# Three-layer forward pass on one core: finer first loads and another order of small work at the seams and in the last layer

## The chip, the cores and the metric

The kernel runs on one core of one Trainium2 chip. The metric is the device time of one execution in microseconds. The core has TensorE (PE, matmuls), VectorE (DVE), ScalarE (ACT), GpSimd (POOL) and SyncE (SP), which run side by side and wait for each other through semaphores; SP and POOL start transfers that 16 DMA engines carry out.

## The reference

One batch, T = 256 positions, width D = 2048, everything in f32. Two blocks of the form

```
h = rmsnorm(x, g0);  m = mixer(h);  x = x + rmsnorm(m, g1)
h = rmsnorm(x, g2);  f = relu(h @ w1)^2 @ w2;  x = x + rmsnorm(f, g3)
```

The first block's mixer is `z = h @ w_in` (2048 to 6144), a short convolution over three columns, a long two-sided convolution with filters that a small network makes (`sin` of `emb @ w1`, `@ w2`, `@ w3`, times a window), gates, and `@ w_out`. The second block's mixer subtracts centred means and multiplies by four 512x512 weights. The third layer is a hybrid attention: after a norm, one wide product gives the inputs of 8 MLA heads (low-rank queries and keys, rotary part), 4 NSA heads (compressed, selected and windowed keys) and 4 heads that attend to a memory of 256 rows. Each head's output is multiplied by `silu(z)`, the 16 heads' 2048 columns go through `w_out_2`, and the sum with x, scaled by a last norm, is the output.

## The kernel before, in words

All of the weights, some 400 MB, stream through the core once, as tiles of 128x2048 f32 (1 MB), which SP loads in the order of use into a ring of `NS = 4` slots raw0 to raw3 (`load_tile`, L962). ScalarE rounds a tile to its high part hi (L484), VectorE subtracts and keeps the low part raw_r (L604), and TensorE multiplies the columns of x, which are split in high and low too, in three products per pair: hi·high, hi·low, low·high (L341). A tile of 512 output columns gives 24 matmuls of 128x512: 4 rows of blocks (k), 2 halves of the positions (t), 3 products. `gemm` (its loop ends at L1152) runs them; `take` and `release` load the tile four ahead and split the tile `AHEAD = 2` further on.

Everything that isn't a product of weights is put between the products by hand. Small functions stand in the lists `later` and `extra`; `step()` calls the next one, at each tile's end and, with `steps=2`, after the second k as well. A function that is called there emits its instructions on every engine at that point of each engine's program. `release(j)`, which stands ahead of that step, emits the split of the tile further on first, unless `hold` says otherwise: then the split is emitted by the next `take`, behind the step's work. In `gemm` a true `hold` holds the last tile of a product alone.

Parts that the change touches:

- The start (L1373 to L1449). TensorE multiplies zeros (`warm`, the count is 4; each product of zeros is two matmuls in the profile) until the first data come. SP loads blocks of x^T (`first_block`, tile R_g) and the first two weight tiles in halves (`first_tile`, `load_piece`, L965). ScalarE and VectorE make for each block of 128 rows first the column of x (R_h<-R_g,cols: L480, L591), then the quarter tile (raw, 128x512). `last_rows` waits for x and issues the filters' tables on POOL (semaphore c6: w_f3, c_win and c_dft, 2 MB together).
- The seams, where one layer's sum becomes the next one's x: `x_columns` (L1244) with `residual` (L1350). With P a product in PSUM, the residual gives X (L591, 128x512 pieces), TensorE turns X (L344), ScalarE and VectorE scale the turned blocks into R_h, high part and low part. The first weight tile of the next layer is split in quarters between these (`quarter`). `gained(t)` multiplies the fourth piece of the sum with its gain (R_m, L588). The seams come at about 402 us (the first block's MLP) and 1908 us (the last layer), each time with the same calls.
- The last layer. Products w_i3 to w_i6 give the heads' inputs; the products w_i9, w_i10, w_i7 and w_i8 (`z_group`, L2091) give silu(z). Between them the heads are computed in steps, each head in three parts over three steps: scores (P<-R_s,R_f and the like), maximum and exponential (DVE L853 and L591 with masks, L858 without; ACT L557, L564), turns of them (L344, EV), a copy (ACT L480), values, and the scaled output R_m (DVE L591). `cmp_out` finishes the compressed keys.
- The last product, `w_o2`, reads the heads' gated outputs, turned by TensorE four heads at a time in the order `blocks` (L2266), the same as the order of its weights' rows.

Of the kernel before, what the change touches and what calls it, by code (L numbers as in the profile page):

```python
# [71 lines left out]
def col(v):  # L72
# [14 lines left out]
    [(4876, 5388)],  # L87
]
Z_ORDER = [8, 9, 10, 11, 2, 3, 4, 5, 6, 7, 0, 1]


def laid_out(i):
    o = dict(shape_constants())
# [27 lines left out]
    wo = i["w_out_2"][0]  # L121
    o["w_o2"] = tile_w(np.concatenate([wo[1024:], wo[:1024]], 0), 512)
    o["x"] = np.ascontiguousarray(i["x"][0].reshape(2, 128, 4, 512).transpose(2, 1, 0, 3))
# [4 lines left out]
    g = i["norm_g"]  # L128
# [347 lines left out]
class Act(Engine):  # L476
# [5 lines left out]
    def split(self, k, d, hi, raw, low, apart=False):  # L482
        self.wait_ge(("loaded", k) if k > 1 else ("loaded", k, d // 2))
        self.e.activation(hi, raw, ACT.Copy).then_inc(*self.inc("high_made", ("high", k, d)))  # L484
# [472 lines left out]
class Sync(Engine):  # L957
# [6 lines left out]
    def load_piece(self, k, d, o, i):  # L964
        self.e.dma_start(o, i).then_inc(*self.landed(f"w{2 * k + d}", ("loaded", k, d)))  # L965

# [24 lines left out]
def conduct(E, plan, listing):  # L991
# [122 lines left out]
    def gemm(name, xh, xl, x_names, nk, c, k0=0, steps=1, hold=False, lead=False, tail=False, late=False):  # L1114
# [19 lines left out]
        for group in groups:  # L1134
# [6 lines left out]
            for ts in turns:  # L1141
                for q, j, wh, wl in blocks:
                    for k in range(4):
                        for t in ts:
                            product(q, j, wh, wl, k, t)
                        if k == 1 and steps > 1:
                            step(steps - 1)
                    if ts[-1] == 1:
                        release(j, done[1], hold and q == n - 1)
                    if steps:  # L1150
                        step()
# [92 lines left out]
    def x_columns(res, th, tl, gain, filler=None):  # L1244
# [41 lines left out]
        if filler is None:  # L1286
# [8 lines left out]
            out_of(1)  # L1295
            quarter(3)
            first, second = early(0)
            first()
            squares_of(1)
            gained(0)  # L1300
            start(1, second)
            fetch(0, (1,))
            fetch(1, (1,))
            fetch(2)
            at_["pause"] = True
# [71 lines left out]
    b, k, warmed = bank(), ev(), mark("warm")  # L1377
    E.warm(b, k, 4, mark("zero"), warmed)
    bank_free[b] = ev_free[k] = [warmed]
    E.halves(half_m)  # L1380

    def first_tile(k, d):
        q = slice(1024 * d, 1024 * d + 1024)
        E.load_piece(k, d, m.raw[k][:, q], a["w_z"][k][:, q])
# [642 lines left out]

    extra += [cmp_last, nop, cmp_sums, nop, nop, cmp_turn, nop, cmp_out]

# [47 lines left out]

    banks, done = gemm("w_i3", HH, HL, h_m, 16, 512, steps=2)
    flush()
# [11 lines left out]
    def z_group(name, n, onto=False, between=None):  # L2091
        banks, done = gemm(name, HH, HL, h_m, 16, 512, steps=2)
        if between is not None:
# [133 lines left out]
    def mla_heads():  # L2227
        def over():
# [9 lines left out]
    banks, done = gemm("w_i4", HH, HL, h_m, 16, 512, steps=2)  # L2238
    flush()
# [5 lines left out]
    later.append(lambda: qnsa_m.extend(turn_plain(ks4, ms4, 128, 4, m.QNSA[:, 0:4, :], 96, [list(kpe_m), list(blk_m.values())], more=vw_m)))  # L2245
    banks, done = gemm("w_i5", HH, HL, h_m, 16, 384, steps=2)
    flush()
# [4 lines left out]
    extra += [lambda h=h: head_step(nsa(h, 1)) for h in range(4)] + [cmp_softmax, head_step, head_step, cmp_turned, lambda: cmp_values(0), lambda: cmp_values(1)]  # L2252
    banks, done = gemm("w_i6", HH, HL, h_m, 16, 512, steps=2)
    flush()
# [10 lines left out]

    blocks = [8, 9, 10, 11, 12, 13, 14, 15, 0, 1, 2, 3, 4, 5, 6, 7]  # L2266

    class Heads:
# [5 lines left out]
        def __getitem__(self, g):  # L2274
            return [o_m[blocks[self.k0 + 4 * g + h], t] for h in range(4) for t in range(2)]

    def heads_of(k0, n, th, tl, after=None):
        return columns(lambda t, c: ZO[:, t, 128 * blocks[k0 + c]:128 * blocks[k0 + c] + 128], Heads(k0), n, th, tl, th_free=after)

# [19 lines left out]
    for g in range(4):  # L2299
# [16 lines left out]
        if g < 3:  # L2316
            for t in range(2):
# [6 lines left out]
SEMAPHORES = (["product_done", "turn_done", "high_made", "act_done", "low_made", "dve_done", "pow_done", "row0", "row1", "stored"]  # L2324
              + [f"ring{k}" for k in range(NS)] + [f"w{k}" for k in range(4)] + [f"xt{c}" for c in (0, 2, 4, 6, 8, 12)] + [f"x{g}" for g in range(4)] + [f"c{k}" for k in range(17)])

# [68 lines left out]
```

## Time and profile before

| | us |
|---|---|
| median of 3 runs | 2354.55 (2353.98 to 2354.76) |
| profiled execution | 2354.21 |
| its span, first to last instruction | 2352.4 |
| TensorE busy | 2337.4 (99%), 10,945 matmuls |
| VectorE busy | 1304.2 (55%) |
| ScalarE busy | 1081.8 (46%) |
| transfers | 446.07 MB, mean 190 GB/s |

The granted clock of TensorE was 0.999 of full over the span. The span is what the timeline and the waits are counted in; the execution's own time is 1.8 us longer. TensorE's record of a matmul includes its pipeline, so records of neighbours overlap; a row "x2" in a timeline is two such that follow each other without a gap. An idle field in brackets is the time in which the engine had nothing to do ahead of the group, with the instruction that ended it.

### The profile page before, as it was taken

How to read it: one execution, taken by the hardware profiler on the slowest of the kernel's cores; microseconds unless marked ns; L12 is line 12 of the kernel's file. 1: busy time of each engine (PE TensorE's matmuls, PEld its weight loads, DVE VectorE, ACT ScalarE, POOL GpSimd, SP SyncE). 2: the span in 40 equal slices, each digit the busy share in tenths (PEclk: the TensorE clock that was granted, in tenths of full speed). 3: DMA queues.
4: the chain of work that ended last, by engine and by line, in shares of the span. 5: the costliest groups of instructions: out<-in, count | busy, mean ns of one | idle time of the engine just before them, and what ended most of it. 6: DMA issues, size and time to landing. Idle time of an engine off the chain costs nothing.

```text
span 2352.4 us, 25298 instructions
## 1 busy us (share of the span) xinstructions
PE 2337.4 (99%) x10945; PEld 1932.0 (82%) x10945; DVE 1304.2 (55%) x1330; ACT 1081.8 (46%) x1174; POOL 27.0 (1%) x46
## 2 busy tenths in 40 slices
PE   9999999999999999999999999999999999999998
PEld 7778788888888888888888888888888888888887
DVE  6655855544544554546864454544544575456654
ACT  6344444544344344354664444344344364444443
POOL 0000000000000000000000000000000010000000
PEclk9999999999999999999999999999999999999999
DMA  8444555655555555555555555555555555644444
GB/s 326 161 161 179 179 198 196 211 183 195 183 212 184 191 188 188 196 180 207 206 197 192 183 192 185 193 186 190 196 180 196 185 177 210 245 161 146 150 153 143
DMA packets 64159, 446.07 MB, mean 190 GB/s; under 512 B 7241, under 2 KB 7572, under 8 KB 12527
## 3 DMA queue, kind: packets, MB, share of 16 engines
q1 hardware_dynamic: 61568, 429.58, 51.6%
q0 software_dynamic: 2336, 14.76, 1.7%
q8 instruction: 86, 1.41, 0.2%
q14 instruction: 25, 0.20, 0.0%
q10 hardware_dynamic: 144, 0.12, 0.0%
HBM read 442.33 MB, written 2.10 MB: 189 GB/s over the span
## 4 chain that ended last, share of the span: by engine, by line
PE 94%; DMA 2%; ACT 2%; DVE 1%; issue 1%; SPq 0%; POOL 0%; ACTq 0%; POOLq 0%
PE P L341 92%; PE P L344 3%; DMA raw<-in_w_i 1%; ACT hi L484 1%; DMA raw<-in_w_z 1%; DVE raw_r L604 1%; ACT EV L510 0%; ACT EV L480 0%; DVE R_m L588 0%; SPq L969 0%; DVE R_h L591 0%; DVE X L591 0%; ACT EV L564 0%; ACT EV L557 0%; ACT R_h L480 0%
## 5 line engine op out<-in xcount | busy, mean ns | idle before, releaser
L604 DVE TENSOR_TENSOR raw_r<-raw,hi 128x2048 fp32r<-128x2048 f32 (+3 forms) x417 | 912.5, 2190 | 946.6 <-ACT hi L484 945.5
L484 ACT ACTIVATE hi<-raw 128x2048 fp32r<-128x2048 f32 (+3 forms) x417 | 763.8, 1833 | 1011.0 <-DMA raw<-in_w_d 388.1
L341 PE MATMUL P<-hi,R_h 128*128 128x512 f32 (+2 forms) x3840 | 1225.0, 393 | 1.5 <-DVE R_h L591 1.1
L341 PEld LDWEIGHTS P<-hi,R_h 128*128 128x128 f32 x3840 | 720.4, 188 | 153.5 <-issue 7.7
L341 PE MATMUL P<-hi,R_f_r 128*128 128x512 f32 x2480 | 776.9, 391 | 0.0
L341 PE MATMUL P<-raw_r,R_h 128*128 128x512 f32 (+2 forms) x1920 | 744.7, 388 | 0.0
L341 PEld LDWEIGHTS P<-hi,R_f_r 128*128 128x128 f32 x2480 | 465.5, 188 | 96.5 <-issue 0.3
L341 PE MATMUL P<-raw_r,R_f_r 128*128 128x512 f32 x1240 | 482.6, 389 | 0.0
L341 PEld LDWEIGHTS P<-raw_r,R_h 128*128 128x128 f32 x1920 | 361.0, 188 | 73.2 <-issue 4.3
L341 PEld LDWEIGHTS P<-raw_r,R_f_r 128*128 128x128 f32 x1240 | 232.9, 188 | 47.5
L344 PE MATMUL P<-ident,EV 128*128 128x128 f32 (+1 forms) x476 | 71.4, 272 | 0.7 <-ACT R_s L480 0.5
L588 DVE TENSOR_TENSOR R_m<-P,R_m 128x512 f32<-128x512 f32 x112 | 71.8, 682 | 0.0
L344 PEld LDWEIGHTS P<-ident,EV 128*128 128x128 f32 (+1 forms) x476 | 58.0, 139 | 14.8 <-issue 2.0
L588 DVE TENSOR_TENSOR R_f_r<-P,R_f_r 128x512 fp32r<-128x512 f32 x66 | 45.0, 684 | 0.0
L540 ACT ACTIVATE EV<-P,st 128x512 f32<-128x512 f32 x64 | 42.8, 669 | 0.0
L542 ACT ACTIVATE EV<-EV 128x512 f32<-128x512 f32 x64 | 40.5, 633 | 2.0
L510 ACT ACTIVATE EV<-X 128x512 f32<-128x512 f32 x48 | 29.9, 633 | 23.2 <-DVE X L588 20.2
L480 ACT ACTIVATE R_f_r<-P 128x512 fp32r<-128x512 f32 x66 | 38.0, 578 | 1.7 <-PE P L344 1.7
L557 ACT ACTIVATE EV<-EV,STAT 128x256 f32<-128x256 f32 (+1 forms) x32 | 14.6, 456 | 51.1 <-DVE STAT L853 51.1
L510 ACT ACTIVATE EV<-R_m 128x512 f32<-128x512 f32 x24 | 15.0, 626 | 34.3 <-DVE R_m L588 34.3
L480 ACT ACTIVATE R_h<-P,cols 128x128 fp32r<-128x128 f32 (+1 forms) x64 | 21.4, 432 | 16.5 <-PE P L344 16.4
L341 PE MATMUL P<-R_f,R_s 65*128 65x512 f32 (+5 forms) x96 | 27.8, 418 | 0.0
(190 smaller groups left out, 768.4 us busy)
## 6 DMA issues: line engine op xcount, KB each, us to landing
raw<-in_w_u SPq DMA_DIRECT2D x128, 1024.0 KB, 4.8
raw<-in_w_d SPq DMA_DIRECT2D x128, 1024.0 KB, 4.8
raw<-in_w_z SPq DMA_DIRECT2D x46, 1024.0 KB, 4.9
raw<-in_w_i SPq DMA_DIRECT2D x36, 1024.0 KB, 4.8
raw<-in_w_mo SPq DMA_DIRECT2D x16, 1024.0 KB, 4.8
raw<-in_w_o SPq DMA_DIRECT2D x16, 1024.0 KB, 4.8
raw<-in_w_mkv SPq DMA_DIRECT2D x8, 1024.0 KB, 4.7
R_g<-in_rows POOLq DMA_DIRECT2D x6, 1024.0 KB, 5.3
```

The source lines that it names most:

```text
L341: return self.e.matmul(o, l, r, start=start, stop=stop, skip_group_check=True)
L344: return self.e.transpose(o, i, self.m.ident[0:i.shape[0], 0:i.shape[0]])
L480: self.e.activation(o, i, ACT.Copy, **scale).then_inc(*self.inc("act_done", done))
L484: self.e.activation(hi, raw, ACT.Copy).then_inc(*self.inc("high_made", ("high", k, d)))
L510: self.e.activation(dst, src, ACT.Square, accum_out=o, **scale).then_inc(*self.inc("act_done", done))
L540: self.e.activation(o, p, ACT.Relu, scale=r).then_inc(*self.inc("act_done", evacuated))
L542: self.e.activation(o, o, ACT.Square).then_inc(*self.inc("act_done", done))
L557: self.e.activation(E[:, o:o + n], E[:, o:o + n], ACT.Exp, bias=S[:, t:t + 1], accum_out=S[:, 2 + t:3 + t]).then_inc(*self.inc("act_done", ...
L588: self.e.tensor_tensor(o, a, b, op).then_inc(*self.inc("dve_done", *done))
L604: self.e.tensor_tensor(low, raw, hi.bitcast(f32), ALU.subtract).then_inc(*self.inc("low_made", *names))
```

## The change

It has five parts. (1) At the start there are three products of zeros in place of four; the first weight tile comes in four quarters of 256 KB, the first of them ahead of x^T, and for this tile the quarter is split ahead of x's column. (2) The filters' tables are issued by a step of their own, one step later, and wait for the ninth weight tile ("loaded", 8) and no longer for x alone. (3) At the seams the fourth weight quarter is split behind the first turned blocks, and `gained(0)` stands behind four pieces of X. (4) In the last layer w_i3 to w_i6 and the z groups are held at every tile (`hold="all"`), and `cmp_out` stands behind the scores of the first MLA head. (5) The heads' order in the last product is NSA, MLA 0 to 3, memory, MLA 4 to 7, where it was NSA, memory, MLA.

```diff
+HEAD_ORDER = [8, 9, 10, 11, 0, 1, 2, 3, 12, 13, 14, 15, 4, 5, 6, 7]
...
-    o["w_o2"] = tile_w(np.concatenate([wo[1024:], wo[:1024]], 0), 512)
+    o["w_o2"] = tile_w(np.concatenate([wo[128 * h:128 * h + 128] for h in HEAD_ORDER], 0), 512)
...
                     if ts[-1] == 1:
-                        release(j, done[1], hold and q == n - 1)
+                        release(j, done[1], hold == "all" or hold and q == n - 1)
...
             out_of(1)
-            quarter(3)
             first, second = early(0)
             first()
+            quarter(3)
             squares_of(1)
-            gained(0)
             start(1, second)
             fetch(0, (1,))
             fetch(1, (1,))
+            gained(0)
             fetch(2)
...
-    E.warm(b, k, 4, mark("zero"), warmed)
+    E.warm(b, k, 3, mark("zero"), warmed)
...
     def first_tile(k, d):
-        q = slice(1024 * d, 1024 * d + 1024)
+        n = 1024 if k else 512
+        q = slice(n * d, n * d + n)
...
-    first_block(0, 0, 2)
     first_tile(0, 0)
+    first_block(0, 0, 1)
+    first_tile(0, 1)
+    first_block(0, 1, 1)
+    first_tile(0, 2)
     first_block(0, 2, 2)
-    first_tile(0, 1)
+    first_tile(0, 3)
...
         first_rows(3)
-        side_load("c6", m.f_w3, a["w_f3"], x_m[3])
+
+    def filter_tables():
+        side_load("c6", m.f_w3, a["w_f3"], ("loaded", 8))
...
         for c in range(4):
-            first_column(4 * g + c)
             q = slice(512 * c, 512 * c + 512)
-            E.split(g, c, m.hi[g][:, q], m.raw[g][:, q], m.low[g][:, q], True)
+            if g == 0:
+                E.split(g, c, m.hi[g][:, q], m.raw[g][:, q], m.low[g][:, q], True)
+                first_column(c)
+            else:
+                first_column(4 * g + c)
+                E.split(g, c, m.hi[g][:, q], m.raw[g][:, q], m.low[g][:, q], True)
...
-    later += [nop, last_rows, half_squares, nop, first_norm]
+    later += [nop, last_rows, half_squares, nop, first_norm, filter_tables]
...
-    banks, done = gemm("w_i3", HH, HL, h_m, 16, 512, steps=2)
+    banks, done = gemm("w_i3", HH, HL, h_m, 16, 512, steps=2, hold="all")
...
-        return [lambda h=h: head_step(mla(h)) for h in range(8)] + [head_step, over]
+        heads = [lambda h=h: head_step(mla(h)) for h in range(8)]
+        return heads[0:1] + [cmp_out] + heads[1:] + [head_step, over]
...
-    blocks = [8, 9, 10, 11, 12, 13, 14, 15, 0, 1, 2, 3, 4, 5, 6, 7]
```

The same `hold="all"` stands in the gemms of w_i4, w_i5, w_i6 and of `z_group`; `Heads` and `heads_of` use `HEAD_ORDER`. The changed kernel's lines stand one and more below those of the kernel before.

Three places show what moved. First SP's queue at the start of the program; raw is the first weight tiles, R_g holds x^T. Before:

```order
L969 DMA R_g<-in_xt 128x512
L965 DMA raw<-in_w_z 128x1024
L969 DMA R_g<-in_xt 128x512
L965 DMA raw<-in_w_z 128x1024
```
and in the changed kernel:

```order
L966 DMA raw<-in_w_z 128x512
L970 DMA R_g<-in_xt 128x256
L966 DMA raw<-in_w_z 128x512
L970 DMA R_g<-in_xt 128x256
L966 DMA raw<-in_w_z 128x512
L970 DMA R_g<-in_xt 128x512
L966 DMA raw<-in_w_z 128x512
L970 DMA R_g<-in_xt 128x512
```
The first 256 KB of weights now stand at the head of the queue, and the blocks of x^T behind them are of one, one and two columns of 256.

Second VectorE at the seam near 1908 us, from the residual's last product on; raw_r is the fourth quarter's low part, R_h the scaled turned blocks, st the sums of squares and the norm. Before:

```order
L588 TENSOR_TENSOR R_m<-P,R_m 128x512
L604 TENSOR_TENSOR raw_r<-raw,hi 128x396
L591 SCALAR_TENSOR_TENSOR R_h<-P,cols,R_h 128x128 x4
L588 TENSOR_TENSOR R_m<-R_m,R_g 128x512
L627 TENSOR_REDUCE st<-st 128x1
L596 TENSOR_SCALAR st<-st 128x1
L591 SCALAR_TENSOR_TENSOR R_h<-P,cols,R_h 128x128 x4
L588 TENSOR_TENSOR st<-st 128x1
L591 SCALAR_TENSOR_TENSOR st<-st 128x1 x2
L591 SCALAR_TENSOR_TENSOR X<-R_m,st,X 128x512 x4
L591 SCALAR_TENSOR_TENSOR R_h<-P,cols,R_h 128x128 x8
```
and in the changed kernel:

```order
L589 TENSOR_TENSOR R_m<-P,R_m 128x512
L592 SCALAR_TENSOR_TENSOR R_h<-P,cols,R_h 128x128 x4
L605 TENSOR_TENSOR raw_r<-raw,hi 128x396
L628 TENSOR_REDUCE st<-st 128x1
L597 TENSOR_SCALAR st<-st 128x1
L592 SCALAR_TENSOR_TENSOR R_h<-P,cols,R_h 128x128 x4
L589 TENSOR_TENSOR st<-st 128x1
L592 SCALAR_TENSOR_TENSOR st<-st 128x1 x2
L592 SCALAR_TENSOR_TENSOR X<-R_m,st,X 128x512 x2
L589 TENSOR_TENSOR R_m<-R_m,R_g 128x512
L592 SCALAR_TENSOR_TENSOR X<-R_m,st,X 128x512 x2
L592 SCALAR_TENSOR_TENSOR R_h<-P,cols,R_h 128x128 x8
```
The quarter went from ahead of the first R_h to behind them, and the second R_m from ahead of the norm to between the X. The seam near 402 us has the same order now; before, its quarter stood ahead of its R_h as well, with no R_m between.

Third VectorE at the memory heads; raw_r is a weight tile's low part, STAT the maxima and sums of the scores, R_m<-P,STAT,R_m a head's output. Before:

```order
L604 TENSOR_TENSOR raw_r<-raw,hi 128x2048
L858 TENSOR_REDUCE STAT<-P 128x2
L596 TENSOR_SCALAR STAT<-STAT 128x2
L864 RECIPROCAL STAT<-STAT 128x2
L858 TENSOR_REDUCE STAT<-P 128x2
L596 TENSOR_SCALAR STAT<-STAT 128x2
L591 SCALAR_TENSOR_TENSOR R_m<-P,STAT,R_m 128x128 x2
L864 RECIPROCAL STAT<-STAT 128x2
L604 TENSOR_TENSOR raw_r<-raw,hi 128x2048
```
and in the changed kernel:

```order
L859 TENSOR_REDUCE STAT<-P 128x2
L597 TENSOR_SCALAR STAT<-STAT 128x2
L865 RECIPROCAL STAT<-STAT 128x2
L605 TENSOR_TENSOR raw_r<-raw,hi 128x2048
L859 TENSOR_REDUCE STAT<-P 128x2
L597 TENSOR_SCALAR STAT<-STAT 128x2
L592 SCALAR_TENSOR_TENSOR R_m<-P,STAT,R_m 128x128 x2
L865 RECIPROCAL STAT<-STAT 128x2
```
Before, the low part stands ahead of the maximum of the next head's scores; now it stands behind that maximum and its reciprocal.

## Rows read from the trace of the kernel before

**Rows 1.** The page, section 1: busy us (share of the span) and instructions of each engine.

```profile
PE 2337.4 (99%) x10945; PEld 1932.0 (82%) x10945; DVE 1304.2 (55%) x1330; ACT 1081.8 (46%) x1174; POOL 27.0 (1%) x46
```

**Rows 2.** TensorE's waits over the whole span: engine, line, releaser, us, times, longest.

```profile
PE P L344 <- DVE R_m L591: 0.9, 1, 0.9
```

**Rows 3.** Timeline of TensorE, 0 to 10 us: start, duration, engine, operation, idle before.

```profile
1.46 3.78 PE L341 MATMUL P<-EV 128*128 128x512 f32 x4 [1.46 <-DVE half L613]
5.03 2.66 PE L341 MATMUL P<-EV 128*128 128x512 f32 x4
7.45 0.47 PE L341 MATMUL P<-hi,R_h 128*128 128x512 f32 x1
```

**Rows 4.** Timeline of VectorE at the start of the program.

```profile
6.61 0.69 DVE L604 TENSOR_TENSOR raw_r<-raw,hi 128x512 fp32r<-128x512 f32 x1 [1.29 <-ACT hi L484]
```

**Rows 5.** Windows of the start: us, busy of each engine, PEclk, DMA share, GB/s.

```profile
5.00:10.00 5.00, 5.00 (x16) 3.04 (x15) 2.99 (x6) 3.19 (x7) 0.35 (x1) 1.00 1.01 364
```

**Rows 6.** Timeline of ScalarE, 16 to 31 us.

```profile
16.70 0.63 ACT L484 ACTIVATE hi<-raw 128x512 fp32r<-128x512 f32 x1 [2.12 <-DMA raw<-in_w_z]
...
26.33 1.90 ACT L484 ACTIVATE hi<-raw 128x2048 fp32r<-128x2048 f32 x1
```

**Rows 7.** Timeline of TensorE, 28 to 32 us.

```profile
30.60 0.50 PE L341 MATMUL P<-hi,R_h 128*128 128x512 f32 x1 [0.23 <-DVE raw_r L604]
```

**Rows 8.** Timeline of TensorE, the first matmul that reads the filters' tables.

```profile
68.86 1.02 PE L341 MATMUL P<-R_f,R_s 65*128 65x512 f32 x2
```

**Rows 9.** Timeline of ScalarE at the two seams.

```profile
401.04 1.14 ACT L480 ACTIVATE R_h<-P,cols 128x128 fp32r<-128x128 f32 x4 [3.46 <-PE P L344]
...
1906.74 1.14 ACT L480 ACTIVATE R_h<-P,cols 128x128 fp32r<-128x128 f32 x4 [2.71 <-PE P L344]
```

**Rows 10.** Timeline of VectorE at the two seams.

```profile
401.69 1.13 DVE L591 SCALAR_TENSOR_TENSOR R_h<-P,cols,R_h 128x128 fp32r<-128x128 f32 x4 [0.83 <-ACT R_h L480]
402.74 0.68 DVE L588 TENSOR_TENSOR R_m<-P,R_g 128x512 f32<-128x512 f32 x1
...
407.85 2.15 DVE L591 SCALAR_TENSOR_TENSOR R_h<-P,cols,R_h 128x128 fp32r<-128x128 f32 x8
...
1907.16 0.56 DVE L604 TENSOR_TENSOR raw_r<-raw,hi 128x396 fp32r<-128x396 f32 x1
1907.64 1.12 DVE L591 SCALAR_TENSOR_TENSOR R_h<-P,cols,R_h 128x128 fp32r<-128x128 f32 x4
...
1913.79 2.15 DVE L591 SCALAR_TENSOR_TENSOR R_h<-P,cols,R_h 128x128 fp32r<-128x128 f32 x8
```

**Rows 11.** Timeline of TensorE at the two seams.

```profile
408.36 0.62 PE L341 MATMUL P<-hi,R_h 128*128 128x512 f32 x2
...
1908.04 0.45 PE L341 MATMUL P<-hi,R_h 128*128 128x396 f32 x1 [0.68 <-DVE R_h L591]
...
1911.94 1.32 PE L344 MATMUL P<-ident,X 128*128 128x128 f32 x8 [0.41 <-DVE X L591]
...
1914.02 0.63 PE L341 MATMUL P<-hi,R_h 128*128 128x396 f32 x2
```

**Rows 12.** Timeline of TensorE in the last layer.

```profile
2099.07 1.05 PE L344 MATMUL P<-ident,EV 128*96 128x128 f32 x8 [0.18 <-ACT EV L480]
...
2205.11 1.47 PE L341 MATMUL P<-R_f,R_s 96*128 96x256 f32 x8
2206.60 0.91 PE L341 MATMUL P<-R_g,EV 128*128 128x128 f32 x6
...
2237.66 1.16 PE L341 MATMUL P<-R_s,EV 128*128 128x128 f32 x8 [0.81 <-ACT EV L480]
...
2253.70 1.06 PE L344 MATMUL P<-ident,R_m 128*128 128x128 f32 x8 [0.89 <-DVE R_m L591]
```

**Rows 13.** Timeline of VectorE at the memory heads.

```profile
2232.97 2.29 DVE L604 TENSOR_TENSOR raw_r<-raw,hi 128x2048 fp32r<-128x2048 f32 x1 [2.89 <-ACT hi L484]
...
2250.74 2.29 DVE L604 TENSOR_TENSOR raw_r<-raw,hi 128x2048 fp32r<-128x2048 f32 x1 [2.19 <-ACT hi L484]
```

More of the change, by code:

```diff
@@ L482, in split @@
     def split(self, k, d, hi, raw, low, apart=False):
-        self.wait_ge(("loaded", k) if k > 1 else ("loaded", k, d // 2))
+        self.wait_ge(("loaded", k, d) if k == 0 else ("loaded", k, d // 2) if k == 1 else ("loaded", k))
         self.e.activation(hi, raw, ACT.Copy).then_inc(*self.inc("high_made", ("high", k, d)))
@@ L964, in load_piece @@
     def load_piece(self, k, d, o, i):
-        self.e.dma_start(o, i).then_inc(*self.landed(f"w{2 * k + d}", ("loaded", k, d)))
+        self.e.dma_start(o, i).then_inc(*self.landed(f"w{4 * k + d}", ("loaded", k, d)))
     def first_load(self, sem, o, i, done):
@@ L2026, in cmp_sums @@
         cmp_silu()
-    extra += [cmp_last, nop, cmp_sums, nop, nop, cmp_turn, nop, cmp_out]
+    extra += [cmp_last, nop, cmp_sums, nop, nop, cmp_turn, nop]
     cq_m = ranked("w_i0", m.CQH, m.CQL, m.gq)
@@ L2091, in z_group @@
     def z_group(name, n, onto=False, between=None):
-        banks, done = gemm(name, HH, HL, h_m, 16, 512, steps=2)
+        banks, done = gemm(name, HH, HL, h_m, 16, 512, steps=2, hold="all")
         if between is not None:
@@ L2233, in over @@
             E.cmp_ready([cmp_m["kv"], list(acc_free)], cmp_m["ready"])
-        return [lambda h=h: head_step(mla(h)) for h in range(8)] + [head_step, over]
+        heads = [lambda h=h: head_step(mla(h)) for h in range(8)]
+        return heads[0:1] + [cmp_out] + heads[1:] + [head_step, over]
     extra += mla_heads()
-    banks, done = gemm("w_i4", HH, HL, h_m, 16, 512, steps=2)
+    banks, done = gemm("w_i4", HH, HL, h_m, 16, 512, steps=2, hold="all")
     flush()
@@ L2245, in conduct @@
     later.append(lambda: qnsa_m.extend(turn_plain(ks4, ms4, 128, 4, m.QNSA[:, 0:4, :], 96, [list(kpe_m), list(blk_m.values())], more=vw_m)))
-    banks, done = gemm("w_i5", HH, HL, h_m, 16, 384, steps=2)
+    banks, done = gemm("w_i5", HH, HL, h_m, 16, 384, steps=2, hold="all")
     flush()
@@ L2252, in conduct @@
     extra += [lambda h=h: head_step(nsa(h, 1)) for h in range(4)] + [cmp_softmax, head_step, head_step, cmp_turned, lambda: cmp_values(0), lambda: cmp_values(1)]
-    banks, done = gemm("w_i6", HH, HL, h_m, 16, 512, steps=2)
+    banks, done = gemm("w_i6", HH, HL, h_m, 16, 512, steps=2, hold="all")
     flush()
@@ L2274, in __getitem__ @@
         def __getitem__(self, g):
-            return [o_m[blocks[self.k0 + 4 * g + h], t] for h in range(4) for t in range(2)]
+            return [o_m[HEAD_ORDER[self.k0 + 4 * g + h], t] for h in range(4) for t in range(2)]
     def heads_of(k0, n, th, tl, after=None):
-        return columns(lambda t, c: ZO[:, t, 128 * blocks[k0 + c]:128 * blocks[k0 + c] + 128], Heads(k0), n, th, tl, th_free=after)
+        return columns(lambda t, c: ZO[:, t, 128 * HEAD_ORDER[k0 + c]:128 * HEAD_ORDER[k0 + c] + 128], Heads(k0), n, th, tl, th_free=after)
     o0_m, parts = heads_of(0, 4, m.OH0, m.OL0)
@@ L2324 @@
 SEMAPHORES = (["product_done", "turn_done", "high_made", "act_done", "low_made", "dve_done", "pow_done", "row0", "row1", "stored"]
-              + [f"ring{k}" for k in range(NS)] + [f"w{k}" for k in range(4)] + [f"xt{c}" for c in (0, 2, 4, 6, 8, 12)] + [f"x{g}" for g in range(4)] + [f"c{k}" for k in range(17)])
+              + [f"ring{k}" for k in range(NS)] + [f"w{k}" for k in range(6)] + [f"xt{c}" for c in (0, 1, 2, 4, 6, 8, 12)] + [f"x{g}" for g in range(4)] + [f"c{k}" for k in range(17)])
 def tensor_program(e, counts, mem, a, out, plan, live):
```

## The prediction

> **What bounds the kernel now.** I read the shares of the engines first, then TensorE's waits, then the timeline around each place that the change touches. TensorE is busy 2337.4 of 2352.4 us [rows 1]: the 10,945 matmuls set the time, and an edit that doesn't alter them can only win or lose waits. There are few: 15.0 us of the span, and the one wait for the vector engine's R_m, 0.9 us, is among the longest [rows 2]. A change of 0.2% is 4.7 us, about what a measurement of this kernel can tell from no change, so a third of everything there is to win would have to go before it shows.
>
> How a wait is priced: a matmul's record of 512 columns is 0.39 us long, but two such take 0.62, so the next starts 0.23 after the one before and their records overlap by 0.16. A wait therefore costs the idle field plus about 0.16.
>
> **The start.** The eight null matmuls start at 1.46, the fifth at 5.03, so 0.89 apart; the first real product starts at 7.45 without an idle field before it [rows 3]. VectorE's first low part, which it needs too, starts at 6.61 and takes 0.69 [rows 4], so nulls and data end together. The high part started some 0.65 before, near 5.95, when the first 768 KB of x^T and weights had landed. The change has 256 KB there, the first weight quarter; 512 KB fewer at 364 GB/s [rows 5] are 1.4 us, so it lands near 4.5. The low part then runs from 5.2 to 5.8, and the column, half a microsecond on each of the two engines, is ready near 6.3. The six null matmuls end one and two of these spacings after the fifth's start: 5.03 + 2 x 0.85 = 6.7. So the first product moves from 7.45 to about 6.7, 0.75 earlier.
>
> None of that reaches the end. ScalarE stands idle for 2.12 us until 16.70, when the third weight tile (tile 2) lands, and from there it works in one row: eight pairs of weight quarter and column, four squares of x, the high part of tile 4 from 26.33 for 1.90 [rows 6]. VectorE's low part takes the 2.3 us after it, and TensorE's product at 30.60 waits for that [rows 7]. Since ScalarE waited for a transfer at 16.70, work done sooner before it changes nothing; the bytes ahead of tile 2 are the same, so it lands when it did. TensorE comes 0.75 earlier and waits 0.75 longer. Three more DMAs on SP and narrower rows could make tile 2 later, and a few tenths in the other direction are as possible: the bounds are -0.39 (the wait of rows 7, 0.23 + 0.16, vanishes) and +0.3. I take 0, for the transfers overlap.
>
> The filters' tables, 2 MB on POOL's queue, wait for the ninth tile instead of x. The ninth has landed when TensorE begins it, at the latest 8 x 24 x 0.227 = 43.6 us after 7.45, at 51; 2 MB at the rate of rows 5 are 5.8 us, so they are there by 57. The first matmul that reads them stands at 68.86 [rows 8], 12 us later. SP's tiles 5 and 6 land sooner, and no product waits there. POOL's power of the norm moves ahead of the three issues, its reader no longer behind anything: 0. Were they later than 68.86, TensorE would wait for all of the excess.
>
> **The seam near 402 us.** ScalarE's first copy to R_h starts at 401.04 and VectorE's at 401.69, 0.65 later [rows 9, 10]. The low part of the last weight quarter (0.6 of pace) stands ahead of this today, in idle time; the change puts it behind the first four R_h, where the R_m of 402.74 (0.68 long, 0.6 of pace) stood, and that R_m goes between the second and third X. So the first two X come when they did, but the eight R_h of the other half, 407.85 now, start at about 408.5. TensorE's group at 408.36 reads the first of them with its second matmul, at 408.59 [rows 11]. First ready at 408.46 + 0.35 = 408.8: **+0.3 us**.
>
> **The seam near 1908 us.** Here the low quarter stands at 1907.16, between R_m and the R_h of 1907.64 for which TensorE's product at 1908.04 waits [rows 10, 11]. With it gone R_h could start 0.48 sooner, but ScalarE's first copy is at 1906.74 [rows 9], and 0.65 behind that is 1907.39: 0.25 won at the first product. The turn at 1911.94, which waits for X, moves hardly: the quarter's high part now delays ScalarE's squares and second copies by 0.44, and X starts at about 1911.05 instead of 1911.13. So the 0.25 turns into a longer wait at the turn, less 0.08. Then the other half's R_h start 0.6 later than 1913.79, and TensorE's group at 1914.02, whose second matmul reads the first of them, waits until about 1914.7 where it went on at 1914.3. **+0.4 us** in all.
>
> **The last layer.** The rule "hold" puts the splitting of the tile ahead behind the step's own work. Four waits have the same cause, a low part of 2.29 us in front of something small:
> - 2099.07: the turn waits 0.18 for ScalarE's copy [rows 12], itself behind an exponential that waited for VectorE: 0.34.
> - 2206.60: this group starts 0.02 after the record of the group at 2205.11 ends, where without a wait it would start 0.16 before: 0.18.
> - 2237.66: values of the first memory head wait 0.81 for a copy, behind the exponential of the next head, behind the low part that starts at 2232.97 [rows 13]: 0.97.
> - 2253.70: the turn of the memory heads' output waits 0.89 for R_m, which stands behind the low part of 2250.74: 1.05. Here the order of heads helps too: the turn that comes first is now that of MLA heads 0 to 3, finished long before.
>
> Sum **-2.5 us**. What do these low parts then make late? A tile is split two tiles, 10.9 us, ahead of its use (AHEAD), and the splits move by the step's own work, under 3 us: nothing. One new wait may come: in a step in the middle of a tile the scores' maximum can now fall behind a low part released at the tile's start; I allow +0.1.
>
> Total: 0 + 0.3 + 0.4 - 2.5 + 0.1 = **-1.7 us**. The profiled execution took 2354.21 us (span 2352.4 and 1.8 around it), so 2352.5; it lies 0.34 below the median of 2354.55, so 2352.85 there. I say 2352.8.
>
> **A rule against it.** TensorE's clock: the first four null matmuls take 3.78 us by their records, the last four 2.66 [rows 3], so the clock went from its 1.2 to its 2.4 GHz level inside that group, around 6.6 us, after TensorE had worked on null products from 1.46 on. The changed kernel works without a gap over the same stretch, only that real products follow at 6.7, so I expect the rise at the same place.
>
> The Trainium skill's page "TensorE: Matmul & The Clock Gate" (Part 1, What's actually happening) has the array at half clock by default, faster only after it has been kept busy, and the moment of the rise varying from run to run. By that rule a null product fewer may meet a data wait and leave real products on the slow level. The trace agrees on the slow start; it shows one rise only.
>
> **The rivals.**
> 1. *The clock rises late* (slower, 5%). If the first quarter's data miss 6.7 and TensorE stands idle there, products run at 0.45 instead of 0.23. TensorE has 0.75 + 0.39 us in hand before the product of 30.60. A tile of 24 matmuls at half speed costs 24 x 0.227 = 5.4, less 1.1: +4.3, which gives 2352.8 + 4.3 = 2357.1. It begins to cost once the slow stretch after the first product passes 2.3 us, and from 5.7 us on the whole is slower than now; two tiles' worth would be over 2360. For it: the null products end just as the data come. Against: hardly any gap.
> 2. *The waits only move* (20%). Low parts held back meet the next step: the values after a held tile wait for an exponential behind the low part, as at 2237.66 today. Half of 2.5 comes back, the seams cost 0.7: -0.5, thus 2354.0. For it: a tile of 5.4 us has two steps, and a split takes 1.9 + 2.3 of it. Against: nothing but the small work is on the path.
> 3. *Everything the change aims at goes* (15%): the seams cost nothing and give 0.25 + 0.5, the start's 0.39 vanishes, the last layer gives 2.6. Sum -3.8: 2350.7.
> 4. *The change does nothing*: only where TensorE's waits were not on the path; it is busy 99%, so each counts. 2%, at 2354.5.
>
> My forecast has 58%. The range of 8 in 10 takes in the second rival and reaches close to the third: 2350.8 to 2354.6. Faster by over 0.2% (below 2349.8) needs more than all of rival 3: 0.03. Slower by over 0.2% (above 2359.3) needs two tiles at half clock, or a late transfer at each seam: 0.02. Within: 0.95.
>
> **What would show it.** In the changed kernel's profile: a first product near 6.7 and TensorE idle for about 0.75 us more before 30.6, whose product still starts at 30.6; R_h of the other halves some 0.6 later at both seams with a wait of 0.3 to 0.4 behind them; no idle field above 0.2 at the memory heads; the wait for R_m gone from the list. I am wrong if 30.6 moves by more than 0.4, if a seam gains, or if the memory heads keep a wait of over half a microsecond.

## The result, and the profile after

The changed kernel took 2357.70 us, median of 20 runs (2355.76 to 2359.28), the kernel before 2354.49 (2353.62 to 2355.95, 20 runs): a ratio of 1.0013, 95% interval 1.0008 to 1.0019. It is 3.2 us slower, where 1.7 us less were forecast. That is inside what the prediction called no change, outside its range, and on the other side.

| | before | after |
|---|---|---|
| profiled execution | 2354.21 | 2357.34 |
| its span | 2352.4 | 2355.5 |
| TensorE busy | 2337.4 | 2338.7 |
| granted clock | 0.999 | 0.998 |

The page of the changed kernel, its span and section 1, which answer to [rows 1]:

```profile
span 2355.5 us, 25298 instructions
...
PE 2338.7 (99%) x10943; PEld 1933.1 (82%) x10943; DVE 1304.7 (55%) x1330; ACT 1081.7 (46%) x1174; POOL 27.0 (1%) x46
```

TensorE has two matmuls fewer (one product of zeros) and is yet busy for 1.3 us more. Its waits over the whole span (columns: total, times, longest) show where the rest went:

```profile
PE P L342 <- ACT R_s L515: 2.4, 1, 2.4
PE P L342 <- DVE raw_r L605: 1.8, 3, 0.8
PE P L342 <- DVE half L614: 1.5, 1, 1.5
PE P L342 <- DVE R_h L592: 1.3, 3, 0.4
PE P L345 <- DVE X L592: 0.6, 1, 0.6
PE P L342 <- DVE R_f_r L592: 0.3, 1, 0.3
```

The wait for R_m [rows 2] is gone, and so are those for the copies EV. On top stands a wait of 2.4 us that the kernel before did not have, for ScalarE's R_s.

**Where the time went.** Both kernels' TensorE queues hold nearly the same instructions, so the start of one and the same instruction in both traces gives the delay so far. One trace is one execution: the fourteen traces here whose kernel has the start of before differ by up to 0.9 us in when tile 2 lands, so delays under 1 us that hang on a landing are not the change's for certain. TensorE at the start:

```profile
6.79 0.79 PE L342 MATMUL P<-hi,R_h 128*128 128x512 f32 x1
...
19.19 0.47 PE L342 MATMUL P<-hi,R_h 128*128 128x512 f32 x1 [0.83 <-DVE raw_r L605]
...
31.59 0.50 PE L342 MATMUL P<-hi,R_h 128*128 128x512 f32 x1 [0.69 <-DVE raw_r L605]
```

The first product comes 0.66 us earlier than in [rows 3], at 6.79 against the forecast 6.7. The one that waits for tile 4 stands at 31.59 against 30.60 [rows 7]: +1.0, where the prediction had no move (its own sign of being wrong was 0.4). Next, TensorE at the second small product of the filter network, and behind it the window view (PEclk is the granted clock):

```profile
57.05 0.64 PE L342 MATMUL P<-R_s 64*64 64x256 f32 x2 [2.43 <-ACT R_s L515]
...
58.95 1.05 PE L342 MATMUL P<-hi,R_h 128*128 128x512 f32 x2
59.80 0.63 PE L342 MATMUL P<-raw_r,R_h 128*128 128x512 f32 x1
```

```profile
57.00:62.00 5.00, 4.95 (x15) 3.50 (x16) 2.98 (x3) 3.07 (x4) 0.00 (x0) 0.68 0.38 159
```

It waits 2.43 us for the sine. From 58.7 us on products are 0.42 apart instead of 0.23: the clock has gone from its 2.4 to its 1.2 GHz level behind the wait, and the mean of 57 to 62 us is 0.68. Down to 62 us this place costs 4.0 us in all, 2.4 of it in the wait and 1.7 in the slow products behind it. The seams, with the first product of before and then those of the changed kernel:

```profile
402.10 0.50 PE L341 MATMUL P<-hi,R_h 128*128 128x512 f32 x1 [0.45 <-DVE R_h L591]
```

```profile
407.02 0.50 PE L342 MATMUL P<-hi,R_h 128*128 128x512 f32 x1 [0.44 <-DVE R_h L592]
...
1913.35 0.45 PE L342 MATMUL P<-hi,R_h 128*128 128x396 f32 x1 [0.45 <-DVE R_h L592]
...
1917.43 1.32 PE L345 MATMUL P<-ident,X 128*128 128x128 f32 x8 [0.56 <-DVE X L592]
...
1920.29 0.45 PE L342 MATMUL P<-hi,R_h 128*128 128x396 f32 x1 [0.45 <-DVE R_h L592]
```

407.02 stands 4.92 behind its partner at 402.10, with the same wait; a few microseconds on, past 414, TensorE is 5.55 behind. At the second seam, against [rows 11]: 1913.35 is 5.31 behind its partner, 1917.43 is 5.49 behind, and 1920.29 is 6.09 behind the second matmul of the group at 1914.02, which started at 1914.20. The last layer:

```profile
2103.92 1.04 PE L345 MATMUL P<-ident,EV 128*96 128x128 f32 x8
...
2241.30 1.05 PE L342 MATMUL P<-R_s,EV 128*128 128x128 f32 x8
...
2246.49 1.13 PE L342 MATMUL P<-R_s,EV 128*128 128x128 f32 x8
...
2255.63 1.91 PE L345 MATMUL P<-ident,R_m 128*128 128x128 f32 x16
```

2103.92 is 4.85 behind its partner at 2099.07, 2241.30 is 3.64 behind 2237.66, and at the end 3.1 are left. Added up: start +1.0, filter network +4.0, first seam +0.6, second +0.5, last layer -2.1, and -0.9 at 1940 and 2046, which is 3.1. The -0.9 is not the change's work. Most of it is a turn at 1935.27 of the kernel before that waits 0.52 for ScalarE's R_s, behind the high part of a tile that has just landed; the wait is gone in the changed kernel, gone in e5 too and 1.26 in e8, and both have the code of before there.

**Why ScalarE was late.** Its timeline, first the kernel before (rows that the prediction did not look at), then the changed kernel:

```profile
42.43 1.92 ACT L484 ACTIVATE hi<-raw 128x2048 fp32r<-128x2048 f32 x1 [4.72 <-DMA raw<-in_w_z]
...
49.91 0.42 ACT L514 ACTIVATE R_s<-R_s 64x256 f32<-64x256 f32 x1
50.23 1.90 ACT L484 ACTIVATE hi<-raw 128x2048 fp32r<-128x2048 f32 x1
```

```profile
42.19 1.92 ACT L485 ACTIVATE hi<-raw 128x2048 fp32r<-128x2048 f32 x1 [1.03 <-DMA raw<-in_w_z]
...
53.36 1.91 ACT L485 ACTIVATE hi<-raw 128x2048 fp32r<-128x2048 f32 x1 [8.77 <-DMA raw<-in_w_z]
55.29 1.28 ACT L515 ACT_TABLE_LOAD   x1
56.59 0.42 ACT L515 ACTIVATE R_s<-R_s 64x256 f32<-64x256 f32 x1
57.56 1.92 ACT L485 ACTIVATE hi<-raw 128x2048 fp32r<-128x2048 f32 x1 [0.56 <-DMA raw<-in_w_z]
```

Before, it makes the sine (R_s, behind a load of its function table of 1.28) at 49.9 and then the high part of the next tile. After, the order is the other way round: the high part of tile 9 comes first, waits 8.77 us for its transfer, and the sine stands behind it at 56.59. TensorE's small product needs it at 50.85 before and at 54.5 after. Two things meet. POOL issues the tables at 42.45, when tile 8 has landed:

```profile
42.45 0.61 POOL L955 DMA_DIRECT2D R_f<-in_w_f  x1 [9.49 <-DMA raw<-in_w_z]
...
43.61 0.54 POOL L955 DMA_DIRECT2D R_s<-in_c_dft  x1
```

and SP issues tile 9 at 43.3, behind the first 1.5 MB of them and just ahead of the last half MB. In the transfers from 43 to 55 us (packets, MB, share of the 16 engines) the tables' queue 0 has more than the weights' queue 1:

```profile
q0 software_dynamic: 395, 2.09, 54.1%
q1 hardware_dynamic: 241, 1.84, 38.5%
```

Tile 9 lands at 53.3, ten microseconds after its issue. (The tables delay a tile in the kernel before as well: issued from 28.87 on, they leave ScalarE idle for 4.72 us ahead of the tile at 42.43. No small operation stands behind that one, and TensorE waits for nothing there.) And `filter_tables` is a step of its own, so every later step, the sine's among them, comes one later, behind the split that it stood ahead of.

### The profile page after: what moved, and what is told of

Read it like the earlier page. It is cut to its first block, busy times and chain, and to the rows that moved or that the text cites. A ratio compares the mean times of both kernels' runs of the same rounds, so it can differ in the third digit from the quotient of the medians.

```text
span 2355.5 us, 25298 instructions
## 1 busy us (share of the span) xinstructions
PE 2338.7 (99%) x10943; PEld 1933.1 (82%) x10943; DVE 1304.7 (55%) x1330; ACT 1081.7 (46%) x1174; POOL 27.0 (1%) x46
## 4 chain that ended last, share of the span: by engine, by line
PE 96%; ACT 1%; DMA 1%; DVE 1%; SPq 0%; issue 0%; ACTq 0%; POOLq 0%; POOL 0%
PE P L342 94%; PE P L345 3%; DMA raw<-in_w_z 1%; ACT hi L485 0%; ACT EV L511 0%; DVE X L592 0%; DVE raw_r L605 0%; ACT R_h L481 0%; SPq L970 0%; DVE R_h L592 0%; SPq L966 0%; ACT EV L481 0%; ACT R_f_r L481 0%; ACT L515 0%; DVE R_m L589 0%
## 5 line engine op out<-in xcount | busy, mean ns | idle before, releaser
L342 PEld LDWEIGHTS P<-raw_r,R_f_r 128*128 128x128 f32 x1240 | 232.9, 188 | 47.5
```

What stands on the lines that cost most here:

```text
L342: return self.e.matmul(o, l, r, start=start, stop=stop, skip_group_check=True)
```

## The experiments

Each run was measured beside the kernel before, in four groups with a median of before each (2354.27, 2354.83, 2354.50 and 2354.84), and the 95% interval of a single ratio reaches about 2 us either way. By these intervals e3, e6 and e10 are slower than the kernel before, e12 and e15 are faster, and e4 just touches no change; the other ten can't be told from it by their times. What is below 2 us is therefore read from the waits in the traces, with the medians beside it.

### The four parts apart

```diff
 e1: the changed kernel with
-later += [..., first_norm, filter_tables]     ("loaded", 8)
+        side_load("c6", ..., x_m[3])           in last_rows, as before
 e2: before with the start's edit    e3: before with the tables' edit
 e4: before with the last layer's edit    e8: before with the seams' edit
```

> The changed kernel with the filters' tables issued as before (behind x, ahead of the norm). Theory T (the tables' 2 MB, issued at 42.5 us, hold up weight tile 9, ScalarE's high part of it stands ahead of the sine, and TensorE waits 2.4 us and then runs 3.4 us at the 1.2 GHz level): the product P<-R_s near 57 us waits no more, clock steady, 4.0 us less than the changed kernel, so about 2353.6. Rival S (the later landing of the first tiles alone is to blame): still 2357.5.

Measured: 2354.66 against 2354.27 (ratio 1.0001, 0.9992 to 1.0009). The wait for R_s is gone, the clock 0.999 in all 11 runs. Of 3.2 us lost, 2.8 came from the tables by the medians, so rival S falls. Theory T's 4.0 put this run at 2353.6, and it is 1.1 higher, which is inside the interval.

> The kernel before with the start alone changed (quarters, three null products, quarter split ahead of the column). Theory T: tiles 2 and 3 land 1.0 us later (17.7 and 21.5), the waits at about 19 and 31.5 us grow, +1.0 us: 2355.5. Rival C (what the prediction took): it comes out even at the product of 30.6, 2354.5.

Measured: 2355.08, +0.8 (ratio 1.0005, 0.9996 to 1.0013). The direction is theory T's, and the interval holds both theories; in its trace the product of 30.60 stands at 30.81, 0.2 later and not 1.0. One run of the eleven took 2360.0 with a clock of 0.998; the others lie between 2354.4 and 2355.9. No trace shows where that one lost its 5 us.

> The kernel before with the tables' step alone changed (own step, wait for the ninth tile). Theory T: +4.0 us, 2358.5, with tile 9 landing some 10 us after its issue where it took 6, a wait of about 2.4 us for ScalarE's sine and a stretch at half clock behind it. Rival I (it needs the late start of the other part as well): under +1 us.

Measured: 2358.79, +4.5 (ratio 1.0016, 1.0007 to 1.0025). Theory T holds, and rival I falls: the start's edit is not needed. The runs come in two kinds: three with a mean clock of 0.999 at 2356.0 to 2356.7, eight with 0.998 at 2358.0 to 2359.9. The first kind loses about 2 us, the second 3.7 to 5.6. The trace is of the second kind: a wait of 2.87 us for the sine, then slow products that cost 1.7. The three runs of the first kind have no trace, so it is open whether they had the same wait with the clock kept, or a shorter one.

> The kernel before with the last layer alone changed (hold at every tile, compressed keys behind the first head, order of heads). Both theories: -2.3 us by the differences of the two traces there (-0.3, -0.3, -1.05, +0.3, -0.7 and -0.2 at 2046), 2352.2; the wait for R_m and that for EV at the memory heads are gone. If the gains were only the late clock's doing: 2354.5.

Measured: 2352.40, -1.9 (ratio 0.9991, 0.9982 to 1.0000). The trace has the same differences as that of the whole change, -0.3, -0.3, -1.05, +0.3 and -0.7; both waits at the memory heads are gone. The sum of these five is -2.1.

> The kernel before with the two seams' edits alone. Theory T: by the traces +0.56 at 402 us and -0.22 + 0.78 at 1908, together +1.1: 2355.4. Rival: the seams were only late because of what came before them, 2354.3.

Measured: 2355.33 against 2354.83, +0.5 (ratio 1.0003, 0.9995 to 1.0012); in the trace TensorE falls behind by 0.6 at the first seam and 0.5 at the second, as in the changed kernel. So by the trace theory T's +1.1 holds and the seams' delay does not need what came before them; the medians show half of it and can't tell it from nothing.

### What makes the tables costly

```diff
 e5: a step of its own, but
+        side_load("c6", m.f_w3, a["w_f3"], x_m[3])
 e7: c_win (1 MB) stays behind x in last_rows; w_f3 and c_dft (1 MB) wait for ("loaded", 8)
 e9: the tables' edit, and
-        banks, done = gemm("w_z", HH, HL, h_m, 16, 512, steps=2, hold=n == 0)
+        banks, done = gemm("w_z", HH, HL, h_m, 16, 512, steps=2, hold="all")
```

> The kernel before with the tables in a step of their own (one step later, behind the norm's power) that still waits for x alone and not for the ninth tile. Theory T (the wait for tile 9 puts 2 MB ahead of the next tile just where ScalarE's sine is due): no cost, 2354.3. Rival P (the step's shift of the filter network against the tiles does it): +4, 2358.8 as with the whole edit.

Measured: 2354.20 against 2354.83 (ratio 0.9998, 0.9989 to 1.0007). The shifted step costs nothing by itself. ScalarE in its trace:

```profile
48.22 1.92 ACT L484 ACTIVATE hi<-raw 128x2048 fp32r<-128x2048 f32 x1 [0.37 <-DMA raw<-in_w_z]
...
51.45 0.42 ACT L514 ACTIVATE R_s<-R_s 64x256 f32<-64x256 f32 x1
```

The sine stands behind the high part of tile 9 here too, but the tile has landed by 48.22, and TensorE, which needs the sine at 53.87, waits for nothing.

> The tables' edit with the window's table (1 MB of the 2) left behind x as before; only w_f3 and c_dft wait for the ninth tile. Theory T: tile 9 lands about 2.5 us earlier, near 50.4, the wait for the sine shrinks from 2.9 to 0.4 or less and the clock stays: 2354.5 to 2355. Rival P (the shift of steps): 2358.8.

Measured: 2355.73, +0.9 (ratio 1.0005, 0.9996 to 1.0013), clock 0.999 in every run. ScalarE in its trace:

```profile
51.16 1.92 ACT L484 ACTIVATE hi<-raw 128x2048 fp32r<-128x2048 f32 x1 [7.01 <-DMA raw<-in_w_z]
...
54.38 0.42 ACT L514 ACTIVATE R_s<-R_s 64x256 f32<-64x256 f32 x1
```

Half the bytes: tile 9's high part begins at 51.16 instead of 52.9 in e3, and TensorE's wait is 1.1 us instead of 2.9. The wait follows the bytes, somewhat less than was expected.

> The tables' edit alone, and the gemms of w_z held at every tile, so that ScalarE's first sine stands ahead of the split of tile 9 again (it is behind it in the changed kernel by the step that the tables took). The 2 MB still land ahead of tile 9. Theory O (the order on ScalarE's queue together with the late tile): the sine runs near 44 us, no wait, clock steady, 2354.5. Rival V (the 2 MB of transfers alone starve TensorE): 2358.8.

Measured: 2354.66 against 2354.50 (ratio 1.0001, 0.9992 to 1.0010), clock 0.999 throughout. This is the run that decides. ScalarE in it:

```profile
43.85 1.91 ACT L484 ACTIVATE hi<-raw 128x2048 fp32r<-128x2048 f32 x1
...
47.07 0.42 ACT L514 ACTIVATE R_s<-R_s 64x256 f32<-64x256 f32 x1
53.31 1.91 ACT L484 ACTIVATE hi<-raw 128x2048 fp32r<-128x2048 f32 x1 [5.82 <-DMA raw<-in_w_z]
```

Tile 9 is as late as ever (its high part starts at 53.31 behind 5.82 us of waiting), yet the sine is done at 47.5, since it stands ahead of the split. TensorE's product at 54.15 waits for nothing. (`hold` stands at every tile of w_z here, so more orders change than this one; the span is 2352.6 us, where the kernel before has 2352.4.) e5 has the order without the late tile, e9 the late tile without the order, and neither costs anything; the small operation queued behind the late tile does.

### The clock behind the wait

```diff
 e6, e10: the tables' edit, and on TensorE ahead of the second filter product
+        for k in range(8): self.mm(P[b][0:64, 0:256], m.f_w1, m.f_emb, True, True)          (e6)
+        for k in range(11): self.mm(P[b][:, :], m.HH[:, k, 0:128], m.hi[3][:, 0:512], ...)  (e10)
         self.wait_ge(ready)
```

> The tables' edit alone (2358.8), with eight repeats of the first small filter product put into TensorE's wait for the sine (result unchanged). Theory T with the clock's part: the wait of 2.9 us stays, filled, but the clock keeps its upper level, so the products behind it run at full speed: 1.6 us less, 2357.2, no stretch at 0.5. Rival: the clock's fall costs nothing, 2358.8.

Measured: 2360.33 against 2354.83, +5.5 (ratio 1.0023, 1.0013 to 1.0033). A miss: it costs more than it saves. The small matmuls took longer than the wait (4.1 us in the profiled execution). That execution and one more of the nine have a mean clock of 0.999 and took 2357.8 and 2358.0; the other seven have 0.997 or 0.998 and took 2359.2 to 2361.7. None of the seven has a trace, so where their clock fell is not shown.

> The tables' edit alone, with eleven full matmuls of 128x128 by 128x512 (2.5 us at full clock, result unchanged) in TensorE's wait for the sine in place of the small ones. Theory: a well filled wait keeps the 2.4 GHz level in nearly all runs, so the loss is the wait alone, 2.3 to 2.9: 2357.0. Rival (nothing put there keeps it, or the clock's fall costs nothing): 2358.8 or more.

Measured: 2357.94 against 2354.50, +3.4 (ratio 1.0014, 1.0005 to 1.0023), clock 0.999 in all eleven runs. TensorE in it:

```profile
53.30 2.88 PE L341 MATMUL P<-hi,R_h 128*128 128x512 f32 x12
56.64 0.64 PE L341 MATMUL P<-R_s 64*64 64x256 f32 x2 [0.46 <-ACT R_s L517]
57.21 0.50 PE L341 MATMUL P<-hi,R_h 128*128 128x512 f32 x1
```

The wait is filled, 0.46 us are left idle, and the products behind it are 0.23 apart. So the fall of the clock can be kept off. What that is worth is less sure: 1.1 us by the medians of two groups (+3.4 against +4.5), 1.7 by the slow products in e3's trace. The expected 2357.0 was 0.9 too low. The wait is as long as in e3 (the small product comes 3.3 us behind the start of the product ahead of it in both), and a second wait shows up: the turn at 60.73 waits 0.49 for ScalarE's copy EV, which stands behind the late splits too and which e3's slow stretch covers.

### The start and the seams

```diff
 e13: weights first, three null products, quarter split first, but loads in halves:
+    first_tile(0, 0)      (512 KB)
     first_block(0, 0, 2)
 e14: quarter(3) behind first(), gained(0) left in its place
 e11: 
-            start(0, lambda: quarter(2))
+            start(0, lambda: (quarter(2), quarter(3)))
```

> The start with the new order (weights ahead of x^T, quarter split ahead of the column, three null products) but the first weight tile still in halves and x^T in pairs of blocks, so no more transfers than before. If the number and size of the transfers cost the 0.8 us of the start's edit: 2354.4. If the order or the missing null product costs it: 2355.2.

Measured: 2354.60 against 2354.84 (ratio 1.0000, 0.9991 to 1.0009), so the first alternative by the medians. ScalarE's first split of tile 2 starts at 16.53, with quarters (e2) at 16.94 and in the changed kernel at 17.69:

```profile
16.53 0.63 ACT L484 ACTIVATE hi<-raw 128x512 fp32r<-128x512 f32 x1 [2.18 <-DMA raw<-in_w_z]
```

```profile
16.94 0.63 ACT L484 ACTIVATE hi<-raw 128x512 fp32r<-128x512 f32 x1 [2.10 <-DMA raw<-in_w_z]
```

The kernel before has 16.70 [rows 6], and the thirteen other traces with its start 16.24 to 17.13 (mean of the fourteen 16.70), so a single trace can't tell half a microsecond. The three with quarters have 16.94, 17.19 (e1) and 17.69, in the mean 0.6 later, and only the changed kernel's lies far outside. That more and smaller transfers are the cause is the better reading, and not shown beyond the noise. The same trace holds a second thing: TensorE at the start and its clock from 3 to 11 us.

```profile
1.46 4.46 PE L341 MATMUL P<-EV 128*128 128x512 f32 x6 [1.46 <-DVE half L613]
7.80 0.51 PE L341 MATMUL P<-hi,R_h 128*128 128x512 f32 x1 [1.89 <-DVE R_h L591]
```

```profile
3.00:11.00 8.00, 6.11 (x13) 3.44 (x12) 4.34 (x9) 4.94 (x11) 1.58 (x3) 0.82 0.97 350
```

The null products ended early, TensorE stood idle for 1.89 us, and the clock went back to the lower level, 0.82 in the mean. By 9.6 us TensorE was 1.9 behind the kernel before; the product of 30.60, which waits no more, was 1.5 behind, and 1.1 were left at the end. This execution took 2355.3, against a median of 2354.6 for the run.

> The seams with the fourth quarter behind the first turned blocks and gained(0) left in its place. By the prediction's reading the eight R_h of the other half are later by the quarter's pace at both seams either way, and here the first X too: +0.9 to +1.3, 2355.6. If gained(0)'s new place were the costly half of the edit: 2354.3.

Measured: 2355.42 against 2354.84, +0.6 (ratio 1.0002, 0.9993 to 1.0011). The median is that of e8, where gained(0) moved too. The traces split it more finely: at the first seam this one falls behind by 0.6 as e8's does, so the quarter's place does all of it there; at the second it falls behind by 0.24 where e8's does by 0.54, so there the new place of gained(0) seems to cost the other 0.3.

> The kernel before with the seams' fourth quarter split one place earlier (with the third, while the first norm's power is on its way) and gained(0) left. Theory: VectorE's stretch ahead of the X at 1908 is 0.48 us shorter, so 0.3 to 0.4 us come off there and nothing at 402: 2354.1. Rival: the norm's wait is short and the quarter delays it, 2354.6.

Measured: 2354.54 against 2354.50 (ratio 0.9999, 0.9990 to 1.0008). No gain that can be told; in the trace TensorE is 0.2 ahead at 1908.

### The last layer, and the combination

```diff
 e15: hold="all" and the new place of cmp_out     e16: HEAD_ORDER alone
 e12: e4 + e5 + e11
```

> The last layer with hold and the compressed keys' place, the heads' order as before. From the differences of the traces hold takes the gains at 2101, 2208 and 2239 (-0.3, -0.3, -1.05, +0.3); the turn of the memory heads at 2254 waits for R_m only if hold doesn't free it too: between 2353.2 (order needed) and 2352.5 (hold alone does all).

Measured: 2351.93 against 2354.84, -2.9 (ratio 0.9989, 0.9981 to 0.9998). TensorE's waits:

```profile
PE P L341 <- DVE raw_r L604: 2.1, 4, 0.9
...
PE P L341 <- DVE R_h L591: 1.1, 2, 0.6
PE P L344 <- DVE X L591: 0.4, 1, 0.4
```

The two others in its list are those for half and R_f_r that every kernel here has; no wait for R_m and none for EV is left. Its trace has the same five differences in the last layer as e4's, -2.1 in sum, so the heads' order adds nothing. `hold` and the place of `cmp_out` were not tried apart; all the waits that went are of the kind that `hold` aims at.

> The last layer with the heads' order alone. It takes away the turn that waits for R_m at 2253.7, 1.05 by the prediction: 2353.4. If the turn of heads 0 to 3 waits in its place: 2354.4.

Measured: 2353.91, -0.9 (ratio 0.9997, 0.9988 to 1.0006). The order alone takes away a part of the same wait (0.5 of 0.9 for R_m is left, and the trace gains 0.3 there), not the 1.05 expected, and adds nothing to what e15 has.

> The last layer's edits, the tables in a step of their own but waiting for x, and the early fourth quarter; start and seams' gained as before. All that won or cost nothing together: -1.9 - 0.3 - 0.3 from 2354.5: 2352.0.

Measured: 2351.96 against 2354.50, -2.5 (ratio 0.9990, 0.9981 to 0.9999). It beats both kernels, by 2.5 and 5.7 us. Since e15 reaches the same, its edit (`hold` with the place of `cmp_out`) is what the gain rests on.

## Why the prediction was wrong

- **The filters' tables, costed at 0: the step that failed.** It named the matmul at 68.86 [rows 8] as the one that could wait, and asked only whether the tables would come too late for it. They don't: the last of them lands near 57, as it said. What it left out is what they do to the rest. They stand ahead of tile 9 in the transfers, and their step pushes ScalarE's sine behind tile 9's split. The sum's term was 0; the trace has +4.0, the edit alone +4.5 (e3). The other terms were too low as well, each by 1 us or less: in the trace they add up to 0.0 (1.0 + 0.6 + 0.5 - 2.1) where the sum has -1.7. The prediction followed the new step past POOL's power ("its reader no longer behind anything") and not past the other steps of the same list, nor on ScalarE's queue. Two rows would have shown it: the sine starts at 49.91, 0.9 us ahead of the small product at 50.85, and a tile's split follows it at 50.23.
- **The start, 0 with bounds -0.39 and +0.3.** The first product's move was right (6.79 against 6.7), and so was that nothing of it would reach the end. The tile that decides came 1.0 later in that trace, 0.2 in e2's. The edit alone measured +0.8, over the upper bound and not clear of noise. "The transfers overlap" was assumed and not read.
- **The seams, +0.3 and +0.4.** Right in sign, and in cause but for one part: the other halves' R_h, in the changed kernel

```profile
406.61 1.12 DVE L592 SCALAR_TENSOR_TENSOR R_h<-P,cols,R_h 128x128 fp32r<-128x128 f32 x4 [1.30 <-ACT R_h L481]
...
413.61 2.15 DVE L592 SCALAR_TENSOR_TENSOR R_h<-P,cols,R_h 128x128 fp32r<-128x128 f32 x8
...
1919.89 2.15 DVE L592 SCALAR_TENSOR_TENSOR R_h<-P,cols,R_h 128x128 fp32r<-128x128 f32 x8
```

  start 7.0 us behind the first R_h at the first seam, where it was 6.2 [rows 10], and TensorE's product at 1920.29 waits 0.45 for them. In size +0.6 and +0.5 by the trace, +0.5 together by e8's median. At the first seam the prediction had the first X unmoved. They come 0.25 later, 5.17 behind where TensorE is 4.92 behind; before and after:

```profile
405.19 2.74 DVE L591 SCALAR_TENSOR_TENSOR X<-R_m,st,X 128x512 f32<-128x512 f32 x4
```

```profile
410.36 1.42 DVE L592 SCALAR_TENSOR_TENSOR X<-R_m,st,X 128x512 f32<-128x512 f32 x2
```

  The quarter's high part moved on ScalarE too, to 406.97, ahead of its second copies; the prediction counted that delay at 1908 and not at 402. The turn of X and the products behind it lose 0.2 by it, the rest is the wait for R_h.
- **The last layer, -2.5 + 0.1.** The four waits went as forecast: -0.34 at 2104, -0.27 at 2211 (0.18 forecast), -1.05 at 2241 (0.97), -0.73 at 2258 (1.05). The new wait came too, and by the way that was forecast, +0.32 at 2246.5 where 0.1 were allowed: the values of the second memory head wait for an exponential, which waits for a maximum behind the low part of 2241.7. In sum -2.1 there against -2.4. Measured alone: -1.9 (e4), -2.9 (e15), the same within their intervals. That no order of heads was needed was not foreseen.
- **The rival "the clock rises late"** had a real mechanism at the wrong place. Its 2357.1 is near the measured 2357.7 by luck: in the changed kernel's trace TensorE has no idle field from 1.46 us until 19.19, and only the first two real products are slow. At the start the fall happened in e13's profile. Of the reserve of 0.75 + 0.39 only the 0.4 of the wait at 30.60 was there, since the first product was not early, and 1.1 us were left at the end. In the changed kernel it came behind the wait at 57 us, where TensorE has no reserve.
- The rise of the clock did not stay in its place, as the prediction expected. The six matmuls of zeros take 5.49 us in the changed kernel and in e1, and 4.46 in e2 and e13; in the changed kernel the first two real products, at 6.79 and 7.38, are still 0.59 apart. The Trainium skill's page "TensorE: Matmul & The Clock Gate" (Part 1, What's actually happening) has the moment of the rise varying from run to run, and these traces agree. What the prediction took from that page, that a gap matters at the start, was too narrow; a gap of 2.4 us in the middle did it.

## What to carry to other kernels

When an edit inserts a step into a hand-made list, compare the order of every engine on both sides of it, and look for small operations that change places with an operation that waits for a transfer: an engine that works in order passes the transfer's lateness on to whatever stands behind it. Before a side load is issued in front of a stream's next tile, ask which queue waits for that tile first, and what stands behind it there. And a rule of the kind "small work ahead of work that is needed two tiles later" (`hold`) paid in both places where it was tried: with the place of `cmp_out` it took 2.1 us off the last layer, and it made the tables' edit harmless (e9). It is not free: one new wait of 0.3 us came with it.

## What the runs showed of the hardware

- Idle stretches of TensorE of 2.43 us (the changed kernel) and 2.87 us (e3) were followed by 3.3 and 3.5 us at the 1.2 GHz level in the two traces. By the mean clock (0.998 or less against 0.999) 8 of the 11 runs of e3 are of this kind, none of 11 with eleven full-size matmuls in the gap (e10), and 7 of 9 with small ones (e6).
- An idle stretch of 1.10 us at the same place was not followed by a fall in e7's trace, and the mean clock was 0.999 in all of its 11 runs.
- A gap of 1.89 us behind the matmuls of zeros at the start was followed by the lower level (e13, 0.82 over 3 to 11 us), one of 0.91 us was not (e2, 1.00, with the products behind it 0.23 apart).
- The granted clock of the windows doesn't show the slow start: it reads 1.00 from 0 to 8 us in the changed kernel, where the matmuls of zeros are 0.85 apart behind the first, twice the 0.43 of the last ones in e2 and e13. The spacing shows it.
- A weight tile of 1 MB that is issued among 2 MB of tables on another queue landed after 10.0 to 10.5 us (the changed kernel, e3, e9), among 1 MB after 8.7 (e7), and after 4.8 to 6.1 in the same stretch of the kernel before: the two queues' packets took 54.1% and 38.5% of the same 16 engines.
